# One 32-step pipeline for both kinds of heads, and rounding remainders beside the attentions moved from GpSimd to VectorE

## The reference, cut to what matters

```python
for i in range(2):                                   # first_block
    h = h + 0.5 * g1 * swiglu(rmsnorm(h) * (1 + sc1) + sh1, ...)
    u = rmsnorm(h, norm_g[i, 1]) * (1 + sc2) + sh2
    mix = hybrid_mixer(u, ...) if i == 0 else mla_mixer(u, ...)
    h = h + g2 * mix                                 # mix ends in a product with w_out
    h = h + 0.5 * g3 * swiglu(rmsnorm(h) * (1 + sc3) + sh3, ...)

def hybrid_mixer(u, positions, w_in, b_f, w_out):
    fq, fk, fv, ff, dq, dk, dv, iq, iw, ik = split(u @ w_in)
    out_a = fox_attention(fq, fk, fv, log_sigmoid(ff + b_f))    # 8 heads of 64: causal, with decay
    out_b = dsa_attention(rope(dq), rope(dk), dv, iq, iw, ik)   # 8 heads of 64: 128 keys picked per token
    return concatenate([out_a, out_b]) @ w_out

for l in range(2):                                   # second_block
    u = rmsnorm(x) @ w_in[l]
    mix = concatenate([mlstm(u), diff_attention(u), hgrn2(u)])
    x = x + mix @ w_out[l]
    x = x + square(relu(rmsnorm(x) @ w_up[l])) @ w_down[l]
```

## Time and profile before

| | us |
|---|---|
| median of 3 runs | 3710.76 (3710.5 to 3712.93) |
| the profiled execution | 3708.42 |
| its span, first to last instruction | 3706.6 |
| what lies around the span | 1.82 |

### The profile page before, as it was taken

One profiled execution on the slowest core, in us unless ns is written; L12 is line 12 of the kernel. 1 busy time (PEld: TensorE's weight loads), 2 busy tenths in 40 slices (PEclk: granted clock), 3 DMA queues, 4 the chain that ended last, 5 costly groups with the idle time before them and its releaser, 6 DMA issues.

```text
span 3706.6 us, 41386 instructions
## 1 busy us (share of the span) xinstructions
PE 3537.7 (95%) x16456; PEld 2785.3 (75%) x16456; DVE 1423.0 (38%) x2526; ACT 1006.5 (27%) x1222; POOL 1603.5 (43%) x565
## 2 busy tenths in 40 slices
PE   8999999789999999998899999978999999789999
PEld 7878777478887888765788876845888869448887
DVE  4454277724243423235201136763201267632010
ACT  2222222522123212203222243342212233422221
POOL 3444451135454545411354554413546545025453
PEclk9999998989999999999999999978999999789999
DMA  6434221024342434221123221201222212002222
GB/s 251 181 142 179 100 82 58 1 80 190 122 191 99 182 130 152 85 63 42 68 80 107 88 99 68 80 1 46 88 94 101 92 68 80 12 28 88 101 92 78
DMA packets 53867, 360.66 MB, mean 97 GB/s; under 512 B 5968, under 2 KB 6352, under 8 KB 16592
## 3 DMA queue, kind: packets, MB, share of 16 engines
q1 hardware_dynamic: 53712, 358.53, 26.4%
HBM read 356.41 MB, written 2.10 MB: 97 GB/s over the span
## 4 chain that ended last, share of the span: by engine, by line
PE 88%; DVE 6%; issue 2%; ACT 2%; POOL 1%; DMA 1%; SPq 0%; DVEq 0%; ACTq 0%; POOLq 0%
PE LP L483 78%; PE XB L483 9%; POOL w_lo L1572 1%; DVE S L2042 1%; PE XB L686 1%; PE LP L802 1%; DMA big<-w_ada 1%; ACT E L1130 1%; DVE tmp L2164 0%; DVE st L2162 0%; ACT w_hi L1130 0%; DVE gain L1878 0%; ACT big_r L1130 0%; ACT sq L1130 0%; DVE wk L2062 0%
## 5 line engine op out<-in xcount | busy, mean ns | idle before, releaser
L1572 POOL TENSOR_TENSOR w_lo<-ring,w_hi 128x2048 fp32r<-128x2048 f32 (+1 forms) x263 | 1125.7, 4280 | 693.5 <-ACT w_hi L1130 693.0
L483 PE MATMUL LP<-u_hi,w_hi 128*128 128x512 f32 x2480 | 986.0, 398 | 17.7 <-ACT u_hi L1130 10.6
L483 PE MATMUL LP<-u_hi,w_lo 128*128 128x512 f32 x2480 | 974.0, 393 | 0.0
L483 PE MATMUL LP<-u_lo,w_hi 128*128 128x512 f32 x2480 | 945.5, 391 | 0.0
L483 PE MATMUL LP<-big_r,w_hi 128*128 128x512 f32 x2432 | 749.5, 389 | 1.2 <-POOL w_lo L1572 1.2
L1130 ACT ACTIVATE w_hi<-ring 128x2048 fp32r<-128x2048 f32 (+1 forms) x263 | 468.7, 1782 | 831.7 <-PE LP L483 739.6
L483 PE MATMUL LP<-big_r,w_lo 128*128 128x512 f32 x1472 | 576.4, 392 | 0.0
L483 PEld LDWEIGHTS LP<-u_hi,w_hi 128*128 128x128 f32 x2480 | 471.1, 190 | 132.5 <-issue 35.9
L483 PEld LDWEIGHTS LP<-u_hi,w_lo 128*128 128x128 f32 x2480 | 470.8, 190 | 100.9
L483 PEld LDWEIGHTS LP<-u_lo,w_hi 128*128 128x128 f32 x2480 | 468.4, 189 | 95.5 <-issue 0.5
L483 PEld LDWEIGHTS LP<-big_r,w_hi 128*128 128x128 f32 x2432 | 455.8, 188 | 95.6 <-issue 1.2
(11 more groups left out here) (303 smaller groups left out, 3648.4 us busy)
## 6 DMA issues: line engine op xcount, KB each, us to landing
ada_in<-w_ada SPq DMA_DIRECT2D x66, 1024.0 KB, 4.9
ring<-w_in SPq DMA_DIRECT2D x22, 1024.0 KB, 4.7
ring<-w_gu00a SPq DMA_DIRECT2D x11, 1024.0 KB, 7.0
ring<-w_gu00b SPq DMA_DIRECT2D x11, 1024.0 KB, 6.8
ring<-w_gu01a SPq DMA_DIRECT2D x11, 1024.0 KB, 6.7
ring<-w_gu01b SPq DMA_DIRECT2D x11, 1024.0 KB, 6.7
ring<-w_gu10a SPq DMA_DIRECT2D x11, 1024.0 KB, 6.7
ring<-w_gu10b SPq DMA_DIRECT2D x11, 1024.0 KB, 7.1
```

The source lines that it names most:

```text
L483: return pe.matmul(o, lhsT=lhsT, rhs=rhs, start=start, stop=stop)
L1572: gp.tensor_tensor(w_lo[:, slab % RING, 0:width], ring[:, slab % RING, 0:width], w_high(q, width).bitcast(F32), ALU.subtract).then_inc(s(" ...
```

## The change

1. One `duo_attention` of 32 steps takes both kinds of heads; scores, bias and values are picked by the pair's number. The pipeline no longer drains between step 15 and step 16.
2. Beside the attentions and the weighted stages, all rests of `hybo`, `mlao`, `wo0`, `wo1` that GpSimd made (eight or six head outputs and the first two slabs of each) are made by VectorE, in pieces of 128 x 512: `rest_mixed` and `quarter_rest`. ScalarE makes the high parts of those slabs in quarters too (`high_quarter`), two steps ahead. They are counted by two semaphores of their own, `wo_high` and `wo_cut`; all other slabs keep `w_high` and `w_cut`.
3. In the norms behind the four output products VectorE adds the squares of chunks 1 to 5, before it takes the next slab (`squares_before`); chunk 6 is summed by TensorE directly (4 more narrow products). GpSimd keeps only the rests of the next two slabs (`weights_only`).

```diff
@@ TensorE @@
+                if pl.wo:
+                    pl.got("h_squared", DC - 1)
+                    for b in range(NB):
+                        mm(XB[1][:, b:b + 1], square_home(DC - 2, late)[:, blk(b)], cc("ones", 0, 1), start=False, stop=False)
...
-            duo_attention(FOX_H // 2, fox_scores, lambda hh, b: fv[:, b, 64 * hh:64 * hh + 64],
+            duo_attention((FOX_H + DSA_H) // 2, duo_scores, duo_values,
                           lambda n: spread_gates(4 + n, [LP[0][:, 1, :]]) if n < 4 else None)
-            duo_attention(DSA_H // 2, dsa_scores, lambda hh, b: dv[:, b, 64 * hh:64 * hh + 64])
@@ ScalarE @@
+            def behind_heads(n):
+                if n % NB == 3 and n >= 7 and n < 32:
+                    cut_output("hybo", n // NB - 1)
+                if n in (20, 21, 22, 24):
+                    high_quarter(pl.cut, (20, 21, 22, 24).index(n))
+                if n in (25, 26, 28, 29):
+                    high_quarter(pl.cut + 1, (25, 26, 28, 29).index(n))
...
-                if n in (9, 21):
-                    high(pl.cut + n // 21)
+                if n in (9, 10, 13, 14):
+                    high_quarter(pl.cut, (9, 10, 13, 14).index(n))
+                if n in (17, 18, 21, 22):
+                    high_quarter(pl.cut + 1, (17, 18, 21, 22).index(n))
...
-                    if n in (1, 2):
-                        high(pl.cut + n - 1)
+                    high_quarter(pl.cut + n // 4, n % 4)
@@ GpSimd @@
+            def weights_only():
+                rest(pl.cut)
+                rest(pl.cut + 1)
+                pl.passed("h_squared", DC)
+                pl.passed("sq_added", DC - 3)
...
-            rest_mixed("hybo", 0, 1, 2, 3)
-            rest(pl.cut)
-            rest(pl.cut + 1)
-            rest_mixed("hybo", 4, 5, 6, 7)
             layer("hybo", last=True)
-            ffn("gu01", "dn01", (4, 6))
+            ffn("gu01", "dn01", weights_only)
@@ VectorE @@
+            def quarter_rest(q, i):
+                slab, width = CUT_SLABS[q]
+                pl.got("wo_high")
+                ins = tt(quarter(w_lo[:, slab % RING, :], i), quarter(ring[:, slab % RING, :], i),
+                         quarter(w_high(q, width), i).bitcast(F32), ALU.subtract)
+                if i == 3:
+                    ins.then_inc(s("wo_cut"), 1)
+            def add_squares(chunks, late):
+                h0, a0, o = pl.seen.get("h_squared", 0), pl.seen.get("sq_added", 0), square_home(0, late)
+                for c in chunks:
+                    dve.wait_ge(s("h_squared"), h0 + c + 1)
+                    tt(o, o, square_home(c, late), ALU.add).then_inc(s("sq_added"), 1)
+                    dve.wait_ge(s("sq_added"), a0 + c)
+            def squares_before(k, late):
+                if k:
+                    add_squares(range(max(1, 2 * k - 2), 2 * k), late)
+                if k == WO_N - 1:
+                    dve.nop().then_inc(s("squares_summed"), 1)
...
+            def beside_heads(n):
+                select_beside(n)
+                if n in (16, 17, 18, 21, 25, 29):
+                    rest_mixed("hybo", (16, 17, 18, 21, 25, 29).index(n))
+                if n in (22, 23, 24, 26):
+                    quarter_rest(pl.cut, (22, 23, 24, 26).index(n))
+                if n in (27, 28, 30, 31):
+                    quarter_rest(pl.cut + 1, (27, 28, 30, 31).index(n))
...
+            def rests_beside_heads(n):
+                if n % NB == 1 and n >= 9:
+                    rest_mixed("mlao", n // NB - 2)
+                for q, units in enumerate(((11, 12, 15, 16), (19, 20, 23, 24))):
+                    if n in units:
+                        quarter_rest(pl.cut + q, units.index(n))
...
+                    if n:
+                        quarter_rest(pl.cut + (n - 1) // 4, (n - 1) % 4)
+                    for c in (2 * n - 12, 2 * n - 11) if n >= 7 else ():
+                        rest_mixed(f"wo{l}", c)
+                rest_mixed(f"wo{l}", 6)
+                rest_mixed(f"wo{l}", 7)
...
-                take(f"wo{l}", add2)
+                take(f"wo{l}", add2, lambda k: squares_before(k, True))
```

More of the change, by code:

```diff
@@ L371, in build, with wo_cuts, normal_cuts, quarter @@
             slabs += n
+        BESIDE = [name in HIGH_CHUNKS and k < 2 for name, n, _, _, two in ORDER for k in range(n if two else 0)]
+        def wo_cuts(q):
+            return sum(BESIDE[0:q + 1])
+        WO_N = WIDTH["hybo"][0]
+        def normal_cuts(q):
+            return q + 1 - wo_cuts(q)
+        def quarter(t, i):
+            return t[:, i * T:(i + 1) * T]
         def w_high(q, width):
@@ L585, in total_sum @@
                 pl.norm += 1
+                pl.wo = False
             def spread(late=0):
@@ L1795, in ada_take, with take @@
                 tt(o, XB[3][:, 0:2], b, ALU.add).then_inc(s("ada_done"), 1)
-            def take(name, body):
+            def take(name, body, before=None):
                 n = WIDTH[name][0]
@@ L1802, in one @@
                 def one(k, it):
+                    if before:
+                        before(k)
                     dve.wait_ge(s("lin_done"), at(pl.slab + k + 1, it, RING))
@@ L1996, in add @@
                     ins.then_inc(s(f"lin_taken{p}"), 1)
-                take(name, add)
+                take(name, add, lambda k: squares_before(k, False))
+                pl.wo = True
             def plain(dst0):
@@ L2283, in _ @@
             take("mlav", values_taken)
-            attention(MLA_H, 192.0 ** -0.5, P, chunked, 0)
+            def rests_beside_heads(n):
[4 more added lines that the diff above has]
+                        quarter_rest(pl.cut + q, units.index(n))
+            attention(MLA_H, 192.0 ** -0.5, P, chunked, 0, beside=rests_beside_heads)
+            rest_mixed("mlao", 6)
+            rest_mixed("mlao", 7)
             residual(1, 1, "mlao")
```

95 lines of the change are left out of this document (56 added, 39 removed).

## The result

The changed kernel takes 3676.36 us in the median of four runs (3673.38 to 3681.57), the one before 3710.63 (3709.01 to 3712.93) on the same chip: a ratio of 0.9908, 95% interval 0.9893 to 0.9923, or 34.3 us less. The forecast was 3679.8, with a range of 3668 to 3694. The profiled execution took 3681.57, the slowest of the four, 26.9 less than the profiled one of before, where the forecast had 31.0 less.

What follows compares the result with a forecast made beforehand. TensorE, busy for 95% of the span, was taken to bound the kernel. Terms of -6.2 - 11.6 - 8.2 - 3.6 - 1.4 = -31.0 us took the profiled 3708.4 to 3677.4, as a median 3679.8, range 3668 to 3694.

Steps and rivals of the forecast that it cites:

- Hybrid attention: Third to last copy: merging and taking GpSimd out saves 7.2 us, exposed pieces cost 1.0; sum -6.2, between -7.2 and +2.5.
- exposed pieces: Hybrid attention, steps 18, 22, 26, 30: a VectorE piece outlasts the 0.35 us idle; 0.26 each, 1.0 us in all.
- rival A: Both attentions: all 28 VectorE pieces show on the chain, 17 us come back, 3696; sign: copies 12 us or more apart; chance 0.10.
- MLA attention: First to seventh copy: two stalls of VectorE scalings behind GpSimd go wholly; -11.6 us, between -11.6 and -1.9.
- Norm behind `hybo` and `mlao`: TensorE's sums no longer wait for GpSimd, ScalarE's squares are late next; 4.1 us gained twice, -8.2, at the lower clock.
- Rival C: VectorE's sums of squares are held by GpSimd's slabs; one hold costs nothing, 2 us left; chance 0.05.
- a second hold: On top of the first, another 4.6 us: TensorE waits 2.5 at each of four places, 3690; next GpSimd subtraction only at 782.
- Weighted stages: Without the held addition and product, waits of 1.03 and 0.79 us go; -1.8 per layer, -3.6 in all.
- Norms behind `wo0` and `wo1`: TensorE's wait of 1.67 us goes, four narrow products more take about 0.95; -0.7 each, -1.4, bounds 0 and -3.3.
- B: Behind `hybo` and `mlao`: TensorE's clock stays at its higher level, 9.0 us more gained, 3671; chance 0.14.
- D: VectorE becomes the bound: 80 new pieces, slower if more than 50 come onto the chain, all give 3728; chance 0.03.
- E: VectorE's long scalings are not held by GpSimd, stalls stay, only the norms gain 9.6 us, 3701; chance 0.03.

Runs made afterwards that it cites:

- experiment 8: Changed kernel, but behind `hybo` and `mlao` ScalarE squares chunks 6 and 7 ahead of the second slab's high part and a table load: 3673.51 us.
- experiment 2: Changed kernel, but GpSimd makes the rests beside attentions and weighted stages, each slab's in four pieces of 128 x 512: 3680.6 us.
- the control: The changed kernel run once more, nothing edited: 3676.64 us, ratio 0.9906 to the kernel before.
- experiment 1: Changed kernel, but GpSimd again makes all rests beside attentions and weighted stages, slabs whole at 128 x 2048: 3703.14 us.
- experiment 10: experiment 9 plus the same filler products at the norms between down and up products of the first block: 3663.82 us.
- experiment 4: Changed kernel, but GpSimd sums the squares again behind all four output products, TensorE summing one chunk directly: 3691.43 us.
- experiment 6: Changed kernel, with each of the 70 rests on VectorE made twice: 3685.89 us.
- experiment 9: experiment 8 plus TensorE filling its waits behind `hybo` and `mlao` with 128 x 512 products that nothing reads: 3670.37 us.
- experiment 11: Kernel before, with one edit: GpSimd makes rests of each output product's first two slabs in four subtractions of 128 x 512: 3701.08 us.
- experiment 3: Changed kernel, but two attention calls of 16 steps, so the pipeline drains between fox and DSA heads: 3680.41 us.

## Why the prediction was right

**Hybrid attention: right in size, right for the larger part.** -6.07 against -6.2. Two groups took longer than 11.13, one 11.72 and one 12.20, 1.7 together, where I had 1.0 for exposed pieces; the last group gave 0.5 back. A group above 12 was my sign for rival A, and it came. But in the 11.72 the clock is 1.00 throughout, and in the 12.20 it is not:

```profile
711.00:715.00 4.00, 4.00 (x25) 2.80 (x26) 2.97 (x11) 2.18 (x7) 0.00 (x0) 0.57 0.01 2
```

The same group with the same pieces took 11.13 in experiment 8, at a clock of 1.00, and there the next one took 12.14. So 0.6 us is exposed pieces, and 1.1 is a fall of the clock whose place changes from run to run. It is no mark of the pieces: experiment 2, without any of them on VectorE, has a group of 12.51, with a mean clock of 0.76 and 0.81 in it. I had overlooked the two or three GpSimd remainders of head outputs in the fox part. An instruction of the key selection, 128 x 512, took 1.15 us beside one and takes 0.49 now, and a pair of scalings went from 1.12 to 0.88: 0.9 of the 2.09 us gained between the first and the third copy. The rest of these lies in the clock and is no gain of the change: from 676 to 684 us its mean is 0.50 and 0.67 in the two stretches of 4 us before and 0.64 and 0.94 after, and the control, with the same instructions, has 30.99 us there and not 29.66.

**MLA attention: right.** -11.59 against -11.6, and experiments 1 and 2 show the cause, GpSimd's long subtractions, by bringing it back and by cutting it up.

**Norm behind `hybo` and `mlao`: right.** I had the sums end 7.8 us behind the slab, it is 7.62. What I called late next were ScalarE's squares. They are. I had not seen that a slab's high part and a table load ahead of them, and not the squares themselves, make them late (experiment 8). That the clock would be at its lower level there, which I took from the earlier trace rows, is what set the 4.1 apart from 6.0, and it came (0.50 from 788 to 792).

**Rival C came true, without its price.** VectorE's sum of chunk 1 is held by GpSimd, and the second slab of `hybo` is taken 18.1 us behind the first instead of 10.8:

```profile
765.50 4.16 DVE L1883 TENSOR_TENSOR wk<-wk,sq 128x512 f32<-128x512 f32 x1 [12.45 <-ACT sq L1172]
769.70 1.41 DVE L2068 SCALAR_TENSOR_TENSOR h<-LP,gate,h 128x512 f32<-128x512 f32 x2
...
773.40 1.41 DVE L2068 SCALAR_TENSOR_TENSOR h<-LP,gate,h 128x512 f32<-128x512 f32 x2 [0.18 <-PE LP L500]
```
```profile
764.50 4.61 POOL L1618 TENSOR_TENSOR w_lo<-ring,big_r 128x2048 fp32r<-128x2048 f32 x1 [6.29 <-ACT big_r L1172]
```

The sum ends 0.55 us behind GpSimd, about its own length. The take ends at 771.1, and TensorE wants the buffer at 773.3: the 2 us of slack that I had worked out, and from the first take to the last it is 32.57 us as before. A second sum, ahead of the fourth slab, is held for 4.68 us in the same way, with about 3 us to spare. My reason against a second hold, that the next subtraction starts only at 782, was taken from the old order; it now starts at 775.38. By the Trainium skill ("SBUF — State Buffer", section "Who interferes with whom") a VectorE instruction with two SBUF inputs contends with a GpSimd instruction that reads SBUF, and the pair of ports that they contend for is an exclusive lock. The trace agrees, with 4.16 us here.

**Weighted stages: this step failed.** I took -1.8 per layer and got +0.22 and -1.10, the same in the control to 0.02. The held addition is gone, and with it the wait of 1.03; the wait of 2.53 behind the held product is 1.44. But other waits grew in their place. TensorE's waits for the two weighted tiles (`S` and `ET`) fell from 7.85 to 6.99 us in layer 0 and from 8.35 to 6.99 in layer 1, so 0.9 and 1.4 of the 1.8 went. And the clock, for which the sum had no term here, is lower in layer 0, with a mean of 0.68 instead of 0.71:

```profile
2477.00:2534.00 57.00, 45.28 (x123) 11.77 (x123) 27.89 (x27) 21.53 (x31) 17.11 (x8) 0.71 0.00 0
```
```profile
2453.00:2511.00 58.00, 47.15 (x123) 12.10 (x123) 27.34 (x40) 22.00 (x37) 0.00 (x0) 0.68 0.00 0
```

(The first row is of before.) The 123 products of the window take 1.9 us more. TensorE in this stage of the changed kernel:

```profile
2478.02 0.92 PE L500 MATMUL LP<-big 64*128 64x384 f32 x4
2480.07 1.98 PE L500 MATMUL XB<-S,big 128*64 128x512 f32 x4 [1.13 <-DVE S L2601]
2481.97 3.57 PE L500 MATMUL XB<-S,ada_in 128*4 128x512 f32 x4
```

Before, these took 1.65, 1.97 and 2.90 us, and the wait ahead of the second was 0.39. So that wait is no piece of VectorE in the way: the product ahead of it ran at the higher clock and was done sooner, and the one behind ran at the lower clock. What the removed hold gave in layer 0, TensorE gave back in the clock. The two layers of the changed kernel show its price: with the same waits, layer 0 takes 59.2 us at a mean clock of 0.68 and layer 1 58.1 at 0.71, in the control and experiments 8 and 10 alike; in experiment 4, with 0.5 us less of waits, layer 1 takes 55.4 at 0.75. Why the clock pattern of this stage is what it is, stays open.

**Norms behind `wo0` and `wo1`: right.** -0.79 and -0.99 against -0.7 each, and experiment 4, which takes the new order back, loses 0.97 and 0.92.

**Rivals A, B, D and E.** Of the pieces in the attentions at most 1.7 us show and not 17 (A), VectorE does not bound (D, experiment 6), the change does what it says (E). B did not come true: the clock fell behind `hybo` as forecast, and the first slab there took 12.73 us. What it was priced at, 9 us for both places, is about what filling the waits is worth in the two traces: 8.3 us from experiment 8 to 9.

**The total.** The median came 3.4 us below the forecast, the profiled execution 4.2 above it (-26.8 against -31.0). By the ledger the weighted stages were 2.7 too good, the second norms 0.4 too poor, and the rest of the kernel moved by up to 2.1 us at five places, 1.4 in sum, where I had nothing; the control shows that such places differ between executions of one kernel. That the median lies as near as it does is in part luck: four executions of this kernel spread over 8 us.

## What to carry to other kernels

Look for VectorE instructions that take several times what their form takes elsewhere, and lay GpSimd's timeline beside them; then shorten the one GpSimd instruction before moving work to another engine. In this kernel that gave 12 us alone (experiment 11) and, with the merge and the new norms, came within 3 us of moving the work (experiment 2). A stall of TensorE costs more than its length where it brings the clock down, and of two stalls near each other the second may cost nothing more (experiments 1 and 3). Shortening such a stall can move the fall of the clock into the work behind it instead of removing it (experiment 8). When two runs are compared stage by stage, take the landmarks on the engine that bounds: another engine's next step can be late by its own new work. When a wait is taken away, read the whole queue of the engine that is late next, not only the operation that is waited for.

## What the runs showed of the hardware

- A VectorE scaling or SBUF-to-SBUF addition that meets a GpSimd subtraction ends 0.1 to 0.6 us after it, whether that subtraction has 512 columns (scaling of 1.45 us) or 2048 (4.75, 4.16).
- VectorE subtracts 128 x 2048 in 2.28 us, GpSimd in 4.5 to 4.6.
- Behind a wait of 3.31 us the granted clock was 0.50 at both places; behind one of 1.38 (experiment 8) it was 0.50 at `hybo` and still 1.00 at `mlao`, where it fell 2 us later. Products whose results nothing reads kept it at 1.00 (experiment 9). 16 narrow products took 3.57 us at the lower level and 1.84 at the higher, a slab of 48 products 13.7 us where the clock came back in it and 11.0 at the higher throughout.
- Draining a pipeline at one seam made two groups of steps 5.4 to 6.6 us longer (29.46 against 24.08 and 22.85 in two executions of the changed kernel), with a granted clock of 0.50 to 0.67 from 698 to 710 us.
